# Delta scan: who copies the second head's solved rows out of PSUM

## The reference, cut to what matters

```
def step(state, inp):
    q_c, k_c, u_c, w_c, a_c, gl = inp
    v_new = u_c - einsum('bhck,bhkv->bhcv', w_c, state)
    o_c = einsum('bhck,bhkv->bhcv', q_c, state) + einsum('bhij,bhjv->bhiv', a_c, v_new)
    state = state * gl[..., None, None] + einsum('bhck,bhcv->bhkv', k_c, v_new)
    return state, o_c
```

## Time and profile before

| | |
|---|---|
| median of 3 runs | 2007.79 us (2005.52 to 2007.82) |
| profiled execution | 2010.39 us, its span 2008.6 us |
| TensorE busy | 1977.5 us of the span |
| VectorE, ScalarE busy | 1168.0 us, 851.8 us |
| stage with the scan, 1350 to 1613 us | TensorE 249.8, VectorE 193.4, ScalarE 148.2 us busy of 263.0 |

### The profile page before, as it was taken

One profiled execution on the slowest core, in us unless ns is written; L12 is line 12 of the kernel. 1 busy time (PEld: TensorE's weight loads), 2 busy tenths in 40 slices (PEclk: granted clock), 3 DMA queues, 4 the chain that ended last, 5 costly groups with the idle time before them and its releaser, 6 DMA issues.

```text
span 2008.6 us, 29603 instructions
## 1 busy us (share of the span) xinstructions
PE 1977.5 (98%) x11597; PEld 1624.2 (81%) x11597; DVE 1168.0 (58%) x1940; ACT 851.8 (42%) x1358; POOL 7.9 (0%) x12
## 2 busy tenths in 40 slices
PE   9999999999999999999999999999999899999998
PEld 6776798888888787888888888778778688888887
DVE  6456467534556666567543555867777666424532
ACT  6447644333334454454332333645664633212322
POOL 0000000000000000000000000000000000000000
PEclk9999999999999999999999999999999999999999
DMA  5112122222223211122222224111111122222221
GB/s 193 63 53 84 43 85 90 88 95 105 104 79 110 69 64 64 63 85 84 100 95 101 103 74 145 42 44 44 64 43 44 51 77 103 105 85 104 88 100 63
DMA packets 26991, 165.55 MB, mean 82 GB/s; under 512 B 3200, under 2 KB 3328, under 8 KB 11008
## 3 DMA queue, kind: packets, MB, share of 16 engines
q1 hardware_dynamic: 25872, 161.69, 22.9%
q10 hardware_dynamic: 1008, 2.30, 0.4%
HBM read 160.83 MB, written 2.10 MB: 81 GB/s over the span
## 4 chain that ended last, share of the span: by engine, by line
PE 86%; DVE 6%; ACT 5%; issue 2%; DMA 0%; SPq 0%; DVEq 0%; ACTq 0%
PE bank L508 25%; PE bank L510 24%; PE bank L509 24%; PE bank L1167 2%; PE bank L783 1%; ACT hH L1364 1%; DVE hL L2143 1%; ACT wH L1364 1%; PE bank L991 1%; PE bank L812 1%; PE bank L1015 1%; DVE x L2139 1%; PE bank L801 1%; ACT L1364 1%; PE bank L1253 1%
## 5 line engine op out<-in xcount | busy, mean ns | idle before, releaser
L508 PE MATMUL bank<-hH,wH 128*128 128x512 f32 x1368 | 550.5, 402 | 1.6 <-DVE hL L2105 1.6
L510 PE MATMUL bank<-hH,wL 128*128 128x512 f32 x1368 | 532.9, 390 | 0.0
L509 PE MATMUL bank<-hL,wH 128*128 128x512 f32 x1368 | 531.9, 389 | 0.0
L1364 ACT ACTIVATE wH<-raw 128x2048 fp32r<-128x2048 f32 (+3 forms) x199 | 294.3, 1489 | 116.6 <-PE bank L510 105.1
L508 PEld LDWEIGHTS bank<-hH,wH 128*128 128x128 f32 x1368 | 257.4, 188 | 62.2 <-issue 9.8
L510 PEld LDWEIGHTS bank<-hH,wL 128*128 128x128 f32 x1368 | 257.1, 188 | 54.7
L509 PEld LDWEIGHTS bank<-hL,wH 128*128 128x128 f32 x1368 | 257.8, 188 | 46.1
L2054 DVE TENSOR_TENSOR wL<-raw,wH 128x2048 fp32r<-128x2048 f32 x96 | 219.7, 2289 | 125.4 <-ACT wH L1364 125.4
L508 PE MATMUL bank<-mH,wH 128*128 128x512 f32 (+1 forms) x610 | 232.8, 382 | 0.0
L509 PE MATMUL bank<-mL,wH 128*128 128x512 f32 (+1 forms) x610 | 232.6, 381 | 0.0
L510 PE MATMUL bank<-mH,wL 128*128 128x512 f32 (+1 forms) x610 | 232.6, 381 | 0.0
(11 more groups left out here) (353 smaller groups left out, 2880.6 us busy)
## 6 DMA issues: line engine op xcount, KB each, us to landing
raw<-in_ffn_up SPq DMA_DIRECT2D x44, 1024.0 KB, 4.8
raw<-in_mlp_up SPq DMA_DIRECT2D x16, 1024.0 KB, 4.8
raw<-in_mlp_down SPq DMA_DIRECT2D x16, 1024.0 KB, 4.8
raw<-in_ffn_down SPq DMA_DIRECT2D x16, 768.0 KB, 4.3
raw<-in_odd_in SPq DMA_DIRECT2D x12, 1024.0 KB, 4.8
raw<-in_dn_qkv SPq DMA_DIRECT2D x12, 1024.0 KB, 4.8
raw<-in_ffn_down SPq DMA_DIRECT2D x16, 640.0 KB, 3.9
raw<-in_even_in SPq DMA_DIRECT2D x7, 1024.0 KB, 4.8
```

The source lines that it names most:

```text
L508: mm(out, a, c, start=first, stop=False, skip_group_check=joined)
L509: mm(out, a, d, start=False, stop=False, skip_group_check=joined)
L510: return mm(out, b, c, start=False, stop=last, skip_group_check=joined)
L1364: return nc.scalar.activation(out, in_, func, **kw)
```

## The change

The three copies of ScalarE become four of half the rows. ScalarE keeps the first head's rows: one scaled copy into vBlk and one plain copy into vNew. VectorE gets the second head's rows, in a new function `scan_solved` at slot f = 1, behind `scan_right` and in front of everything else of the slot. Each half has its own event, so TensorE waits for two events before line 1253 and for two before the next matmul.

```
-                pe.wait_ge(*at(f"scan.vd{p}.{n}"))
+                for e in range(2):
+                    pe.wait_ge(*at(f"scan.vd{p}.{n}.{e}"))
                 mm(bank[7][:, 0:2 * P], kTok[:, p % 2, n, :], vBlk[:].rearrange("p e d -> p (e d)"), start=True, stop=True)\
                     .then_inc(*tick("scan_pe", f"scan.kv{p}.{n}"))
-                pe.wait_ge(*at(f"scan.vn{p}.{n}"))
+                for e in range(2):
+                    pe.wait_ge(*at(f"scan.vn{p}.{n}.{e}"))

...
             def scan(p, n):

                 act.wait_ge(*at(f"scan.v{p}.{n}"))
-                for e in range(2):
-                    last = a(vBlk[part(e), e, :], bank[5][part(e), 2 * P:3 * P], ACT.Copy, scale=expo[part(e), p, 1, n:n + 1])
-                last.then_inc(*tick("scan_act", f"scan.vd{p}.{n}"))
-                a(vNew[:], bank[5][:, 2 * P:3 * P], ACT.Copy).then_inc(*tick("scan_act", f"scan.vn{p}.{n}"))
+                rows = part(0)
+                a(vBlk[rows, 0, :], bank[5][rows, 2 * P:3 * P], ACT.Copy, scale=expo[rows, p, 1, n:n + 1])\
+                    .then_inc(*tick("scan_act", f"scan.vd{p}.{n}.0"))
+                a(vNew[rows, :], bank[5][rows, 2 * P:3 * P], ACT.Copy).then_inc(*tick("scan_act", f"scan.vn{p}.{n}.0"))

...
+            def scan_solved(p, n):
+
+                rows = part(1)
+                dve.wait_ge(*at(f"scan.v{p}.{n}"))
+                ts(vBlk[rows, 1, :], bank[5][rows, 2 * P:3 * P], expo[rows, p, 1, n:n + 1], None, ALU.mult)\
+                    .then_inc(*tick("scan_dve", f"scan.vd{p}.{n}.1"))
+                nc.vector.tensor_copy(vNew[rows, :], bank[5][rows, 2 * P:3 * P]).then_inc(*tick("scan_dve", f"scan.vn{p}.{n}.1"))

...
                 for p, n in scans_at(t, 0):
                     scan_right(p, n)
+                for p, n in scans_at(t, 1):
+                    scan_solved(p, n)
                 for p, n in scans_at(t, 2):
                     scan_state(p, n)
```

## The result

Against the kernel before on the same chip the changed kernel took 1.0019 times as long, with an interval of 1.0011 to 1.0027. Its median is 2012.55 us over 10 runs (2009.28 to 2014.53), against 2007.8 us for the kernel before. By the ratio that is 3.8 us more, with an interval of 2.2 to 5.4 us, and the two medians alone, 4.8 us apart, lie inside it. The profiled execution took 2011.35 us with a span of 2009.6 us; the one of before took 2010.39 us with a span of 2008.6 us.

A forecast was written before the change was run, and what follows sets the result against it. TensorE was taken as the bound (86% of the chain), with only its idle time for sale. Losses of 3.5 us less gains of 2.24 made +1.3, so 2007.8 became 2009.1 us; range 2005.5 to 2013.0 us.

The forecast's parts named there:

- the main forecast: Whole kernel: gains and losses at the scan steps net +1.3 us; 2007.0 to 2010.5 us, chance 0.65.
- the rivals: Clock falls to 1.2 GHz once (0.12) or twice (0.06); VectorE late at all nine places (0.09); VectorE copies free (0.08).
- signs of being wrong: (1, 0) and (2, 0) waits shrink, the (p, 6) solves do not wait, or a second stretch at 1.2 GHz shows up.
- Gains: Writes that waited for ScalarE start earlier: (2, 7), (3, 2), (3, 6) 0.38 each, (3, 1), (3, 4), (3, 5) about 0.3; sum 2.24 us.
- (0, 0): Write of this scan step: a weight half keeps VectorE until 1357.70 us, so only 0.2 us of gain is left.
- The pair: VectorE's two new copies per step: 0.28 us each, about 0.6 us of its queue, 19 us in all; bounds 0.3 and 0.8.
- The hand-over: At (1, 0), from VectorE's scaled copy ending at about 1427.88 us to the write starting at 1427.93.
- I take nothing: TensorE's 64 added wait instructions: the two already before line 1257 left no gap, so no cost was counted.
- First kind of loss: VectorE's copies are late themselves, behind a weight half: writes of (1, 0) and (2, 0) 0.3 us later each, 0.6 together.
- (3, 0): VectorE's weight half ends at 1565.88 us, so the write is 0.7 us late and the next read 0.6 us late.
- Second kind: VectorE's copies delay what follows: solves of (0, 6), (1, 6), (2, 6) lose 1.7 us together, and (3, 4) loses 0.6.
- One fall: Clock falls to 1.2 GHz behind one of the roughly 2.0 us waits at (1, 0) and (2, 0): 2010.7 us, chance 0.12.

The follow-up runs named there:

- the second experiment: Against the kernel before, the split made only at (2, 7), (3, 1), (3, 2), (3, 4), (3, 5) and (3, 6): 2006.09 us, ratio 0.9989.
- the seventh experiment: The kernel before with TensorE's two waits of each write (vBlk, vNew) written twice, no work moved: 2008.82 us, ratio 0.9999.
- the fourth: Kernel before, split at six gaining steps, (0, 7), (1, 0), (1, 7), (2, 0); VectorE's copies at (1, 0), (2, 0) before reduce and weight half: 2005.18 us, 0.9984.
- The sixth experiment: Against the kernel before, the split made only at (0, 5), (1, 5) and (2, 5): 2011.27 us, ratio 1.0009.
- the fifth experiment: Against the kernel before, the split made only at (0, 7), (1, 0), (1, 7) and (2, 0), in the change's queue places: 2011.52 us, ratio 1.0012.
- the repeat: The changed kernel, not edited, timed again beside the kernel before: 2011.75 us, ratio 1.0020.
- the third experiment: The changed kernel with ScalarE making all three copies as before at (1, 0) and (2, 0), split at 30 steps: 2009.46 us, ratio 1.0006 to the kernel before.

## Why the prediction came out as it did

The forecast was 2009.1 us, +1.3, with "within 0.2%" as the likeliest. Measured were +3.8 us: inside the range and just within 0.2%. The median itself, 2012.55 us, lies above the 2007.0 to 2010.5 us of the main forecast and near the upper bound of 2013.0, which had been left open for the rivals, so it was in part luck that the range held. The places and mechanisms of gains and losses were right. Several sizes were off, and a rival that had been given little weight came true: a stretch at 1.2 GHz in a new place was also one of the prediction's own signs of being wrong.

- *Gains.* Forecast 2.24 us. The six writes gave 2.0 us, in the change as in the second experiment, where 2.04 was their part of the forecast. (0, 0) gave nothing in place of 0.2: the scaled copy and the hand-over, both longer than assumed (see below), used it up.
- *The pair.* This term was mis-sized: the scaled copy was taken at 0.28 us and takes 0.356; the plain one takes 0.291. At (1, 0) the pair adds 0.71 us to the queue (1.84 against 1.13 us), where 0.6 was forecast: 0.12 in front of the pair and 0.59 from its start to the next operation. At (0, 6) TensorE loses 0.72 by it.
- *The hand-over and the waits.* From the end of the scaled copy at (1, 0) to the start of the write there are 0.14 us (1427.04 to 1427.18), where I had allowed 0.05. The second wait is not the reason: before, with one wait, it was as long (1426.73 + 0.74 = 1427.47 to 1427.62), and it could have been read there. "I take nothing" for the waits holds here. The 0.1 us of the seventh experiment comes where the same event is waited for twice, and the hand-over at (1, 0) is 0.25 us (1424.13 to 1424.38) in the fourth, where ScalarE's half comes last; why it is longer there is open.
- *First kind of loss.* (1, 0) and (2, 0): forecast 0.3 each, measured 0.35 and 0.36, with the mechanism as described, down to the solve that comes 0.4 us earlier. Hoisting the pair turned it round, so its place behind the reduce and the weight half is shown as the cause. (3, 0): forecast 0.6, measured 0.84; for this step no experiment was made.
- *Second kind.* (0, 6) and (1, 6): forecast 0.6 each, measured 0.72 and 0.73. (2, 6): 0.5 and 0.5. (3, 4): 0.6 and 0.6. The sixth experiment shows the first three alone.
- *The sum.* The waits make +1.9 us where +1.3 was forecast; TensorE's idle time in the stage is 15.5 us where 14.5 was. In the prediction's sum of the losses, the pair's price and the hand-over behind it are what was too low.
- *The clock.* "One fall" had a chance of 0.12. In all three profiles with 2.2 us waits at these steps the clock fell behind (2, 0), and it did not behind (1, 0), whose wait is as long; it cost 1.6 us each time. In the nine profiles without such waits, the one of before among them, it did not fall there. The argument against it, that the 1.80 us of the earlier trace rows had another wait close ahead, carried too much weight, though the length of the wait alone does not decide either. The Trainium skill, "TensorE: Matmul & The Clock Gate", section "What's actually happening", ties the granted clock to how busy the engine has been; the traces agree in so far as every fall in this stage stands behind one of its longest waits, but a wait as long at (1, 0) did nothing.

The fall behind the solve of (3, 7) in the profile before is missing after, where the wait is 1.66 us and not 1.80. The stretch of the changed kernel:

```profile
1602.00:1608.00 6.00, 4.34 (x25) 3.50 (x24) 5.26 (x12) 2.06 (x5) 0.00 (x0) 1.00 0.00 0
```

A wait of 1.80 us stands at this solve in three of the twelve profiles: the clock fell in the one before and in the sixth experiment, and stayed at 1.00 in the fifth. Behind the shorter waits at this solve, 1.45 to 1.73 us, it never fell.

*How often it falls.* Only a profile shows where the clock falls, but the mean granted clock is on record for every timed execution, in three decimals. Over the 11 executions of the repeat it averages 0.9972 and over those of the fifth experiment 0.9969, against 0.9979 and 0.9977 for the kernel before on the same two chips. A stretch of 3.4 us at 1.2 GHz takes 0.00085 off the mean of a span of 2008 us. So each of these two kernels goes through nearly one such stretch more per execution than the kernel before; the third experiment, without the 2.2 us waits, has 0.9978. The second and the fourth, without the 1.80 us wait at (3, 7), have 0.9979 like the kernel before beside them. This speaks against a fall behind (3, 7) in most executions of the kernel before, and for leaving it out of the steps.

*What stays open.* That the additional stretch of the timed executions is the one behind (2, 0) is argued, not shown: without it the change and the fifth experiment would be at +1.9 and +0.7 us, each just under its interval. Why the clock falls behind (2, 0) and not behind (1, 0) was not settled. The loss at (3, 0) and the longer wait behind the last solve have no experiment of their own.

## What to carry to other kernels

Here splitting a late step over two engines paid only where the second engine was idle when the work arrived: read for each place what stands ahead of the new instruction in the in-order queue, and what stands behind it and is waited for. The split at every step was a loss and the same split at six steps a gain of 2.2 us; VectorE making all copies at eight steps, with its queue cleared in front of them and behind, was a gain of 7 us. When a wait has been removed, look at the next link of the same recurrence: here it waited for the same weight half. And a long wait on TensorE can cost more than its length: in this stage the clock fell behind five of the nine waits of 1.8 us or more, and behind (2, 0) that cost 1.6 us each time.

## What the runs showed of the hardware

- A VectorE scaled copy of 64 x 128 from PSUM, with the scale read per row from SBUF, takes 356 ns, and a plain copy of the same shape 291 ns, here in 32 instructions each. A pair of them adds 0.71 us to VectorE's queue between a weight half and a convolution tap. A ScalarE copy of 128 columns takes 257 ns with 64 rows, where it took 277 with 128.
- ScalarE and VectorE read two halves of the rows of one PSUM bank at the same time, and ScalarE's scaled copy stayed at 362 ns; at (1, 1) both engines' scaled copies start at 1431.66 us and take 0.36 us.
- 64 more waits on TensorE gave a ratio of 0.9999 [0.9990, 1.0008]. Where a wait that really stops the engine was written twice, the matmul behind it started about 0.1 us later; where the event had long come, it did not move.
- From the end of the last copy that it waits for to the start of the write there are 0.14 us at (1, 0), whether the copy is ScalarE's or VectorE's.
- TensorE's clock fell from 2.4 to 1.2 GHz for 3.4 us behind a single wait of 2.2 us, in three profiles of three, and that cost 1.6 us; one as long, 70 us earlier, left it alone. Behind one of 1.80 us it fell in two profiles of three, and behind the waits of 1.0 to 1.7 us in this stage in none.
